# Prompt attention in a hybrid decoder step: values weighed in two products, and two score rows of each long unit made a unit earlier

## The reference, cut to what matters

```python
s = (jnp.einsum('bqhr,bkr->bhqk', qlb, c_kv)
     + jnp.einsum('bqhp,bkp->bhqk', qrb, k_r)).astype(jnp.float32)
s = jnp.where(kpos[None, :] <= qpos[:, None], s, -jnp.inf)
p = jax.nn.softmax(s, axis=-1).astype(c_kv.dtype)
return jnp.einsum('bhqk,bkr->bqhr', p, c_kv)
...
a = jnp.einsum('bshr,rhv->bshv', o_lat, w_uv).reshape(B, S, MLA_WIDTH)
```

## Time and profile before

| what | before |
|---|---|
| median of 3 runs | 1351.63 us |
| lowest and highest | 1350.63 and 1353.62 us |
| profiled execution, own time | 1352.7 us |
| its span | 1351.0 us |
| instructions | 23850 |
| granted TensorE clock, mean | 0.990 |

### The profile page before, as it was taken

One profiled execution on the slowest core, in us unless ns is written; L12 is line 12 of the kernel. 1 busy time (PEld: TensorE's weight loads), 2 busy tenths in 40 slices (PEclk: granted clock), 3 DMA queues, 4 the chain that ended last, 5 costly groups with the idle time before them and its releaser, 6 DMA issues.

```text
span 1351.0 us, 23850 instructions
## 1 busy us (share of the span) xinstructions
PE 1305.0 (97%) x9362; PEld 1222.5 (90%) x9362; DVE 823.8 (61%) x1241; ACT 513.4 (38%) x902; POOL 428.5 (32%) x279
## 2 busy tenths in 40 slices
PE   6999999999999999999899999999999999999997
PEld 4788988888888558999899999999999999999987
DVE  5874056666656237278934554445545469899976
ACT  5423224666665425123422322223222234544461
POOL 2633325442433015761134444344443400000000
PEclk9999999999999899999999999999999999999998
DMA  9420101000014544730221222212222189757503
GB/s 295 154 60 27 36 20 58 20 17 5 16 67 164 184 164 146 270 115 33 81 66 70 80 87 80 71 65 78 87 80 79 61 311 349 253 184 257 164 1 132
DMA packets 70346, 151.58 MB, mean 112 GB/s; under 512 B 9107, under 2 KB 16659, under 8 KB 69811
## 3 DMA queue, kind: packets, MB, share of 16 engines
q1 hardware_dynamic: 70258, 150.39, 32.7%
HBM read 127.80 MB, written 22.56 MB: 111 GB/s over the span
## 4 chain that ended last, share of the span: by engine, by line
PE 81%; DVE 8%; issue 5%; DMA 3%; ACT 2%; POOL 1%; SPq 0%; POOLq 0%; DVEq 0%; ACTq 0%
PE ps L984 24%; PE ps L985 24%; PE ps L986 24%; PE ps L1200 2%; DMA araw<-in_w_dn 1%; PE ps L1266 1%; DVE x L2093 1%; PE ps L992 1%; DMA ab<-acts 1%; PE ps L1311 1%; POOL rt L783 1%; DVE hL L2147 1%; PE ps L1276 1%; DVE aHL L2768 0%; DVE bHL L2771 0%
## 5 line engine op out<-in xcount | busy, mean ns | idle before, releaser
L953 POOL TENSOR_TENSOR ws<-wraw,ws 128x1024 fp32r<-128x1024 f32 x50 | 124.6, 2492 | 216.4 <-ACT ws L1579 216.4
L984 PE MATMUL ps<-bHL,aHL 128*128 128x272 f32 x616 | 178.4, 290 | 5.4 <-DVE bHL L2771 5.2
L986 PE MATMUL ps<-bHL,aHL 128*128 128x272 f32 x616 | 177.2, 288 | 0.0
L985 PE MATMUL ps<-bHL,aHL 128*128 128x272 f32 x616 | 177.1, 288 | 0.0
L2614 DVE TENSOR_TENSOR bufP<-bufP,ps 128x544 f32<-128x544 f32 x66 | 47.4, 721 | 133.7 <-PE ps L986 131.4
L1579 ACT ACTIVATE ws<-wraw 128x1024 fp32r<-128x1024 f32 x55 | 58.4, 1062 | 174.8 <-PE ps L986 168.9
L984 PEld LDWEIGHTS ps<-bHL,aHL 128*128 128x128 f32 x616 | 116.0, 188 | 7.0 <-DVE bHL L2771 6.9
L985 PEld LDWEIGHTS ps<-bHL,aHL 128*128 128x128 f32 x616 | 116.0, 188 | 0.0
L986 PEld LDWEIGHTS ps<-bHL,aHL 128*128 128x128 f32 x616 | 115.9, 188 | 0.0
L976 POOL TENSOR_TENSOR rt<-ms,mhalf 128x3 f32<-128x3 f32 (+1 forms) x3 | 3.0, 999 | 254.1 <-DVE ms L2801 254.1
L2347 DVE TENSOR_TENSOR pTL<-ps,pTH 128x512 fp32r<-128x512 f32 (+1 forms) x96 | 53.2, 555 | 43.4 <-ACT pTH L1579 42.5
(11 more groups left out here) (371 smaller groups left out, 4514.8 us busy)
## 6 DMA issues: line engine op xcount, KB each, us to landing
araw<-in_w_dn SPq DMA_DIRECT2D x121, 256.0 KB, 3.4
wraw<-in_w_gu SPq DMA_DIRECT2D x44, 512.0 KB, 3.5
cp<-in_cache SPq DMA_DIRECT2D x64, 272.0 KB, 4.7
ab<-acts SPq DMA_DIRECT2D x34, 272.0 KB, 5.0
raw<-in_w_out SPq DMA_DIRECT2D x16, 512.0 KB, 4.5
acts<-bufC SPq DMA_DIRECT2D x22, 272.0 KB, 2.1
xt<-in_x_tok SPq DMA_DIRECT2D x9, 512.0 KB, 6.9
x<-x2s SPq DMA_DIRECT2D x8, 544.0 KB, 6.3
```

The costliest lines, as they stand in the source:

```text
L953: pool.tensor_tensor(w[:, 1, :], w_source(j), w[:, 0, :], ALU.subtract).then_inc(cw_lo, 1)
L984: nc.tensor.matmul(out, wh, xh, start=start, stop=False)
L985: nc.tensor.matmul(out, wh, xl, start=False, stop=False)
L986: return nc.tensor.matmul(out, wl, xh, start=False, stop=stop)
```

## The change

1. The value block of a pair is kept in one tile `hv` with four parts of 64 columns: high of head 0, low of head 0, low of head 1, high of head 1. `product` takes the 128 columns of the unit's head, high and low side by side, as weights, and does two matmuls, with `pTH` and with `pTL`, in place of three. The 64 rows of high values and the 64 rows of low values come out apart, and are added: ScalarE copies the low rows into `aT` (`move_weighed`), then VectorE adds the high rows to it (`add_weighed`, new, in step 2 of the next unit, behind the rest and a reciprocal of that step), and only that frees the bank.
2. Rows 0 and 1 of each long unit from unit 3 on have their scores two units ahead, in the long unit before: in steps 5 and 7 (of units 1, 5, 9 and 13), or in steps 8 and 9 (of units 3, 7 and 11). Rows 2 and 3 stay in the short unit between, and stand in its steps 0 and 1 where they stood in 2 and 3. Unit 0 keeps its order. The reciprocal and the division of row 3 come in step 2 of a short unit, behind the rest of tile 2 and ahead of the addition.
3. `prob_2` is a second buffer for those two rows, used by every second long unit.
4. GpSimd divides the rows in the new order: in a long unit the three rows of the next unit and then the two rows made ahead, in a short unit one row.

```diff
 def row_at(u, kt):
 
-    qi = kt - (4 if u % 4 == 3 else 0)
-    return qi if u + 1 < UNITS and 0 <= qi < 4 else None
+    if u and u % 2 == 0:
+        return (u + 1, 2 + kt) if kt < 2 else None
+    first = 4 if u % 4 == 3 else 0
+    if u + 1 < UNITS and first <= kt < first + 4:
+        return u + 1, kt - first
+    if u % 2 and u + 2 < UNITS:
+        for qi, at in enumerate((8, 9) if first else (5, 7)):
+            if kt == at:
+                return u + 2, qi
+    return None
...
+def invert_at(u, kt):
+
+    return u + 1 < UNITS and kt == (2 if u and u % 2 == 0 else 7 if u % 4 == 3 else 3)
...
-        hvH, hvL = reg.put("hvH", [P, 8, P], F32R), reg.put("hvL", [P, 8, P], F32R)
+        hv = reg.put("hv", [P, 8, 4, VH], F32R)
         prob = reg.put("prob", [P, prob_at(8)])
+        prob_2 = Region(X0, nc.sbuf_usable_end).put("prob_2", [P, prob_at(6) - prob_at(4)])
...
-                if u < UNITS - 1:
+                if u and u % 2 == 0:
+                    normalise(u + 1, (2,))
+                elif u < UNITS - 1:
                     normalise(u + 1)
+                if u % 2 and u + 2 < UNITS:
+                    normalise(u + 2, range(2))
...
-                    mm3(ps[:, 6 + u % 2, c0:512], hvH[:, kt, :], hvL[:, kt, :], pTH[:, x % 4, c0:512],
-                        pTL[:, x % 4, c0:512], kt == 0, kt == nk - 1).then_inc(pv_x, 1)
+                    both = hv[:, kt, 2 * hh:2 * hh + 2, :].rearrange("p s n -> p (s n)")
+                    out = ps[:, 6 + u % 2, c0:512]
+                    nc.tensor.matmul(out, both, pTH[:, x % 4, c0:512], start=kt == 0, stop=False)
+                    nc.tensor.matmul(out, both, pTL[:, x % 4, c0:512], start=False,
+                                     stop=kt == nk - 1).then_inc(pv_x, 1)
...
             def exponential(u, qi):
...
-                if u >= 2 and qi == 0:
+                if u >= 2 and qi == (2 if u % 2 else 0):
 
                     act.wait_ge(pv_x, tr_count(u - 1))
...
-                part = slice(VH * hh, VH * hh + VH)
-                hi(aT[part, p, 512 * blk:512 * blk + 512], ps[part, 6 + u % 2, :]).then_inc(o_free, 1)
+                part, other = slice(VH * hh, VH * hh + VH), slice(VH - VH * hh, P - VH * hh)
+                hi(aT[part, p, 512 * blk:512 * blk + 512], ps[other, 6 + u % 2, :]).then_inc(o_low, 1)
...
+            def add_weighed(u):
+                p, hh, blk = u // 4, u // 2 % 2, u % 2
+                part = slice(VH * hh, VH * hh + VH)
+                x = aT[part, p, 512 * blk:512 * blk + 512]
+                dve.wait_ge(o_low, u + 1)
+                nc.vector.tensor_tensor(x, x, ps[part, 6 + u % 2, :], ALU.add).then_inc(o_free, 1)
...
             def move_turned(u):
                 blk = u % 2
-                for kt in range(4 * (blk + 1)):
+                for kt in range(4 * (blk + 1) + 2):
                     x = tr_count(u) + kt
                     c0 = P * max(0, kt - 4 * blk)
-                    qi = row_at(u, kt)
-                    if qi is not None and kt < 4 * blk + 3 and not row_late(u, kt):
-                        maximum(u + 1, qi)
-                    if qi:
-                        invert(4 * (u + 1) + qi - 1)
-                    dve.wait_ge(t_hi, x + 1)
-                    nc.vector.tensor_tensor(pTL[:, x % 4, c0:512], ps[:, 4 + x % 2, c0:512],
-                                            pTH[:, x % 4, c0:512], ALU.subtract).then_inc(t_free, 1)
+                    row = row_at(u, kt)
+                    late = kt == 4 * blk + 3 or row_late(u, kt)
+                    if row is not None and not late:
+                        maximum(*row)
+                    if row is not None and row[1]:
+                        invert(4 * row[0] + row[1] - 1)
+                    if kt < 4 * (blk + 1):
+                        dve.wait_ge(t_hi, x + 1)
+                        nc.vector.tensor_tensor(pTL[:, x % 4, c0:512], ps[:, 4 + x % 2, c0:512],
+                                                pTH[:, x % 4, c0:512], ALU.subtract).then_inc(t_free, 1)
                     for i in gens_at(u, kt):
                         move_gen(u // 4 + 1, i)
-                    if qi is not None and (kt == 4 * blk + 3 or row_late(u, kt)):
-                        maximum(u + 1, qi)
-                    if qi == 3:
-                        invert(4 * (u + 1) + qi)
+                    if row is not None and late:
+                        maximum(*row)
+                    if invert_at(u, kt):
+                        invert(4 * (u + 1) + 3)
+                    if kt == 2 and u:
+                        add_weighed(u - 1)
```

More of the change, by code:

```diff
@@ L506, in build, with turned_values, prob_row @@
         CONST = 16 * len(const_loads)
+        def turned_values(j):
+            return ps[:, 4 + j, :].rearrange("p (x s n) -> p x s n", x=4, s=2)
+        def prob_row(u, qi):
+            qt = 4 * (u % 2) + qi
+            if qt in (4, 5) and u // 2 % 2:
+                return prob_2[:, prob_at(qt) - prob_at(4):prob_at(qt + 1) - prob_at(4)]
+            return prob[:, prob_at(qt):prob_at(qt + 1)]
         def gw(t, j):
@@ L885, in query_lo, with normalise @@
                                            qH[:, hh, c0:c0 + n], ALU.subtract).then_inc(q_lo, 1)
-            def normalise(u):
-                for qi in range(3):
+            def normalise(u, rows_of=range(3)):
+                for qi in rows_of:
                     r, qt = 4 * u + qi, 4 * (u % 2) + qi
                     n = P * (qt + 1)
-                    row = prob[:, prob_at(qt):prob_at(qt) + n]
+                    row = prob_row(u, qi)
                     pool.wait_ge(s_rc, r + 1)
@@ L1184, in weigh @@
             def weigh(u):
-                blk = u % 2
+                hh, blk = u // 2 % 2, u % 2
                 nk = 4 * (blk + 1)
@@ L1198, in turn @@
                             pe.wait_ge(s_pd, u + 1)
[L1199 to L1201 removed]
+                        last = nc.tensor.transpose(ps[:, 4 + x % 2, P * qi:P * qi + P],
+                                                   prob_row(u, qi)[:, P * kt:P * kt + P], ident[:, :])
                     last.then_inc(t_ready, 1)
@@ L1215, in weigh @@
                         query_key(u // 4 + 1, i)
-                    qi = row_at(u, kt)
-                    if qi is not None and not row_late(u, kt):
-                        score(u + 1, qi)
+                    row = row_at(u, kt)
+                    if row is not None and not row_late(u, kt):
+                        score(*row)
                     if u % 4 == 0 and kt == 0:
@@ L1226, in weigh @@
                         product(kt - 2)
-                    if qi is not None and row_late(u, kt):
-                        score(u + 1, qi)
+                    if row is not None and row_late(u, kt):
+                        score(*row)
             def sample_queries():
@@ L1754, in move_weighed @@
                 act.wait_ge(pv_x, tr_count(u + 1))
-                part = slice(VH * hh, VH * hh + VH)
-                hi(aT[part, p, 512 * blk:512 * blk + 512], ps[part, 6 + u % 2, :]).then_inc(o_free, 1)
+                part, other = slice(VH * hh, VH * hh + VH), slice(VH - VH * hh, P - VH * hh)
+                hi(aT[part, p, 512 * blk:512 * blk + 512], ps[other, 6 + u % 2, :]).then_inc(o_low, 1)
             def move_turned(u):
                 blk = u % 2
-                for kt in range(4 * (blk + 1)):
+                for kt in range(4 * (blk + 1) + 2):
                     x = tr_count(u) + kt
                     c0 = P * max(0, kt - 4 * blk)
[L1763 to L1766, removed]
+                    if kt < 4 * (blk + 1):
+                        act.wait_ge(t_ready, x + 1)
+                        if x >= 4:
+                            act.wait_ge(pv_x, x - 3)
+                        hi(pTH[:, x % 4, c0:512], ps[:, 4 + x % 2, c0:512]).then_inc(t_hi, 1)
                     for i in gens_at(u, kt):
                         move_gen(u // 4 + 1, i)
-                    if (qi := row_at(u, kt)) is not None:
-                        if qi == 0 and u % 4 == 3:
+                    if (row := row_at(u, kt)) is not None:
+                        if row == (u + 1, 0) and u % 4 == 3:
                             query_hi(u // 4 + 1, GEN - 1)
-                        exponential(u + 1, qi)
+                        exponential(*row)
                     if kt == 1 and u:
@@ L2324, in invert @@
                     qt = 4 * (u % 2) + 3
-                    row = prob[:, prob_at(qt):prob_at(qt + 1)]
+                    row = prob_row(u, 3)
                     dve.wait_ge(s_rc, r + 1)
```

17 lines of the change are left out of this document (9 added, 8 removed).

## The result

| what | before | after |
|---|---|---|
| median (runs) | 1352.47 us (4) | 1392.26 us (4) |
| lowest and highest | 1350.63 and 1353.62 | 1389.73 and 1393.54 |
| profiled execution, own time / span | 1352.7 / 1351.0 us | 1389.73 / 1388.0 us |
| mean granted clock | 0.990 | 0.968 |

The ratio is 1.0299 [1.0279, 1.0319]: **39.8 us slower**. The sign was right. The forecast, 1372.5, had half of the loss, and the upper end of the range, 1384, was 8 us short.

What follows compares the result with a forecast made beforehand. TensorE, busy 97% of the span, was taken as the bound. Removed matmuls (-17.6), short-unit waits (+28.7) and smaller terms made +14.9; with +6 for the clock, 1352.7 became 1373.6, forecast as 1372.5 us against the median; range 1358 to 1384.

Steps and rivals of the forecast that it cites:

- The clock's term, +6: Seven short units: clock falls to its lower level in part of them; half of 7 x 1.7 us gives +6.
- The sum of waits and products, +14.9: Attention: removed matmuls, new waits, lost gains, vanished idle and contention together make the kernel 14.9 us longer, before the clock.
- The order of the queues: Short units 2 to 14: one chain across VectorE and ScalarE holds 4.1 us of waits each, +28.7 us for seven.
- the +0.8 line: Units 0 and 15: they keep only part of their gain, since their waits are ScalarE's and VectorE's; +0.8 us.
- Units 4 and 8: GpSimd splits head weights while VectorE divides the 1024 row: +0.4 us each, +0.8 in all; bounds 0 and 1.3 each.
- today's idle, -2: Attention: of today's 5.7 us of idle TensorE, 2 us vanish into the new waits; -2 us.
- The term -17.6: Attention, eight pairs of units: 96 removed matmuls, each worth its issue interval on TensorE, save 17.6 us.
- The bound of 11.9: Upper bound of the clock's cost: all seven short units have a fall, each paid in full; 11.9 us.
- The upper bound for the strided copies: Values' high and low copies write in strides: today's price taken; bound twice that, 8 times some 1.3 us.
- It falls in every short unit: Rival: the clock falls in every short unit, each fall paid in full; 1378.5 us or more, chance 0.2.
- The orders overlap better: Faster rival, short units: only VectorE's own work counts, wait 1.2 us in place of 4.1; 1346 us, chance 0.13.
- the change does nothing: Rival: second product hides in waits what it saves, moved rows change nothing; within 0.2%, chance 0.04.

Runs made afterwards that it cites:

- Experiment 4: Changed kernel, but in short units the 1024-column row's maximum, exponential and division, and the addition, stand behind all four rests; 1346.50 us, ratio 0.9952.
- Experiment 3: Changed kernel with 105 extra unread matmuls of 512 columns in the three waits of each short unit; 1376.56 us, ratio 1.0175 to the kernel before.
- Experiment 1: Kernel before with only the two products, copy and addition; score rows in the order of before; 1346.72 us, ratio 0.9950.
- experiments 5 and 6: Experiment 1 (in 5) and Experiment 4 (in 6) with the addition later, in step 6 of long units; 1346.36 us (0.9943) and 1347.58 us (0.9952).
- experiment 2: Kernel before with only the rows made ahead and the new short-unit order; three products, no addition; 1395.20 us, ratio 1.0323.
- experiment 7: Kernel before with two unread spare additions on VectorE ahead of the last rest of units 2, 6, 10 and 14; 1374.03 us, one run.
- experiment 8: Kernel before with four unread spare additions on VectorE ahead of the last rest of units 2, 6, 10 and 14; 1388.51 us, one run.

## Why the prediction was right in its mechanism and wrong in its sizes

The chain of waits and the fall of the clock behind it were the ones forecast; their sizes were not. The clock's term, +6, measured about +21.7, because a fall was priced at 1.7 us and cost about 3.1, and because all seven came. The sum of waits and products, +14.9, measured about +22.4, in part because a removed product was worth less than its interval. The parts, one by one:

- **The order of the queues: right.** The chain through maximum, exponential, `aT`, tile 2's high part and rest, and then division, addition and tile 3's rest ran as walked, within 0.2 us at its last product. Experiment 4 shows it to be the cause: without it, at the same matmuls, the loss is a gain of 0.5%.
- **The waits as a sum: +14.9 forecast, about +22.4 found.** Experiment 3 has every unit from 1 to 14 but the ninth at nearly full clock; it is 24.6 us over the kernel before in attention, and 2.2 of them are unit 9's clock. The difference of 7.5 us has these parts. *Unit 15* (part of the +0.8 line) was to gain some 0.8 and lost 1.0: its length, 15.2 to 17.1 us over all kernels, doesn't follow its products, and experiment 3 has 3.4 us more of low clock in it and the sample queries than the kernel before; that makes 1.8. *Units 1, 5, 9 and 13*: I had them grow by the two moved rows less eight products and plus 0.15, about 0.9 us; they grew by 1.3, +1.6 in all. *Units 4 and 8*: I took 0.4 of contention for each; against unit 6 they lost 1.5 each, above even my upper bound of 1.3; that makes 2.1. The 2.0 that are left have the size of the line *today's idle, -2*. That is by subtraction: it fits new waits that came on top of the old ones, and no run shows it.
- **The term -17.6 was too large as well.** The issue interval of a removed matmul is its worth only where TensorE sets the pace. I read the share of idle time of all attention (5.7 of 216 us) as proof that it does; but that was a balance: with eight products out of a long unit, TensorE waits for VectorE's rests. Experiment 1 got 6.6 us, and experiments 5 and 6 show that the addition's place isn't what withholds the rest. In the changed order it is the same: with three products (experiment 2) unit 1 takes 15.40 us, with two 14.48, so 0.9 in place of 1.56; unit 7 takes 25.23 us at full clock, and 24.64 in experiment 3, so 0.6. For units 3, 7 and 11 the sum had put such a loss at 0.7 each; for units 1, 5, 9 and 13 it had 0.15.
- **The clock: +6 forecast, about +21.7 found** (44.1 less 22.4). This is the larger error, and it has two factors. I gave each of the seven falls a chance of one half, and all came. And I priced a fall at 1.7 us from the one example in the trace of before, where 3.4 us at the lower level followed a sparse stretch; here they were 6.8 and 10.2 us. The cost is 2.1 to 2.5 us in units 3, 7 and 11, 3.4 to 3.7 in units 5, 9 and 13, and 3.3 in unit 14 (after against experiment 3, for unit 9 against its like). The bound of 11.9 was no bound, since it repeated one sample seven times.
- **What cost nothing.** The upper bound for the strided copies wasn't needed: a rest of the values took 0.69 us before and after, as their high part took 0.60. The addition took 0.67 to 0.69, as priced.
- **The rivals.** "It falls in every short unit" was the case that came, with the words "or more" carrying 14 us. (The Trainium skill, TensorE: Matmul & The Clock Gate, section HAM oscillation, describes just this repetition; units 3, 5, 7, 9, 11 and 13 agree with it, at the costs above, while in experiments 2 and 7 the clock held behind one of the waits.) "The orders overlap better" is refuted by the timeline of unit 6, "the change does nothing" by the ratio. The walk of the faster rival came to life in another form: experiment 4 has no chain in the short units and takes 1346.5.

## What to carry to other kernels

When work is moved between steps of hand-written queues, write down the new order of every queue and look for what now stands *ahead* of the short operations that the busiest engine waits for: a long row's maximum and exponential belong behind them. Price a new wait of TensorE with the time at the lower clock that follows it, 3.4 to 13.7 us here, and not by the wait alone or by one example; if the wait can't be removed, matmuls that nobody reads can be worth their place in it. And an engine that is busy for 97% beside queues that are just in time isn't alone the bound: taking work from it pays until the others hold it up, here for little more than a third of what the intervals promised.

## What the runs showed that I had not expected

- How long the clock stayed low varied. In the changed kernel it was 6.8 us where projections of 512 columns followed, 10.2 us where the 24 value matmuls of 128 columns did, whose interval went from 0.11 to 0.21 us meanwhile. But what follows doesn't settle it: with the same projections behind it, unit 2 of experiment 2 had 3.4 us, and with the same value matmuls unit 8 had 13.7 in experiment 2 and 6.8 in experiment 3. What does was not found.
- Of equal waits of 3.3 us, behind units 2, 6 and 10, two lowered the clock and one did not (experiment 7); 5.9 us did each time (experiment 8).
- A division on VectorE took 2.11 us beside a division on GpSimd, 0.76 us beside nothing. The spare additions of experiments 7 and 8, two operands from SBUF and 1024 columns, took 1.22 us with GpSimd idle (the last of the four) and 2.59 us where a GpSimd division had begun before them (the second). In unit 10 of experiment 8 an addition began first, and there it was GpSimd's division of 896 columns that took 2.66 us in place of 1.68.
- Small waits hide in busy time. Unit 5 of experiment 1 shows 1.28 us of idle TensorE where 0.22 stood before, 1.06 more; but 1.56 us were taken out and the unit grew by 0.18, so 1.74 were lost. The other 0.7 is in the intervals: for instance, the two products of 256 columns start 0.34 and 0.22 us after the matmul ahead of them, where 0.17 and 0.12 are the price, and no bracket tells of it, because the ends of matmuls are modelled.

Best of all kernels run are experiments 1, 4, 5 and 6, at 0.9943 to 0.9952 of the kernel before. They beat the changed kernel by some 3.4% and the kernel before by 0.5%, and can't be told apart: with the queues in a good order, the rows made ahead gain nothing over two products alone.
